# Activations in four parts by token number instead of two, in a float32 encoder kernel on one core

## What is computed

```python
for i in range(2):
    hn = _rms(h, norm_mix[i])
    h = h + (_even_mixer if i == 0 else _odd_mixer)(hn, ...)
    h = h + _conv_ffn(_rms(h, norm_ffn[i]), ...)
return h[:, N_META:]

def _conv_ffn(h, w_up, conv_w, conv_b, w_down):
    u = h @ w_up                      # 2048 -> 2 x 5632
    ...                               # a convolution over 3 neighbouring tokens
    g, val = jnp.split(acc, 2, axis=-1)
    return (jax.nn.silu(g) * val) @ w_down
```

## Time and profile before

| | us |
|---|---|
| time, median of 3 runs | 2368.8 (2368.6 to 2370.28) |
| the profiled execution's own time | 2367.88 |
| its span, first to last instruction | 2366.2 |
| TensorE busy / VectorE / ScalarE / GpSimd | 2335.8 / 1609.0 / 1185.0 / 51.8 |
| span up to the feed-forward part of layer 0 (first product of up00) | 476.4 |
| from there to layer 1 | 735.6 |
| mixer of layer 1 | 440.7 |
| feed-forward part of layer 1, with the output | 713.5 |

### The profile page before, as it was taken

How to read it: one execution, slowest core, us unless ns; L and a number is a source line. 1 busy time by engine, 2 the same in 40 slices (tenths; PEclk the granted TensorE clock), 3 DMA queues, 4 the chain that set the end, 5 groups by cost and what they waited for, 6 DMA issues and landing times.

```text
span 2366.2 us, 50508 instructions
## 1 busy us (share of the span) xinstructions
PE 2335.8 (99%) x19334; PEld 2278.9 (96%) x19334; DVE 1609.0 (68%) x2314; ACT 1185.0 (50%) x1592; POOL 51.8 (2%) x96
## 2 busy tenths in 40 slices
PE   8999999999999999999999999999999999999999
PEld 7999898999999999999999999999999999999998
DVE  5547786687755776577574667776877667766774
ACT  5345655554443544444459634455545445444543
POOL 0000011000000000000011000000000000000000
PEclk9999999999999999999999999999999999999999
DMA  6644465556566556655665544456566666566665
GB/s 194 189 143 130 134 160 139 181 166 206 182 195 190 184 178 197 195 186 184 192 187 159 159 119 121 139 177 198 179 193 197 213 190 197 183 215 189 199 202 163
DMA packets 431596, 420.25 MB, mean 178 GB/s; under 512 B 26130, under 2 KB 430396, under 8 KB 431452
## 3 DMA queue, kind: packets, MB, share of 16 engines
q1 hardware_dynamic: 417536, 415.29, 56.8%
q10 hardware_dynamic: 13932, 3.17, 1.2%
HBM read 416.31 MB, written 2.10 MB: 177 GB/s over the span
## 4 chain that ended last, share of the span: by engine, by line
PE 91%; DVE 4%; ACT 3%; issue 2%; ACTq 1%; DMA 0%; SPq 0%; DVEq 0%
PE ps L1533 28%; PE ps L1531 25%; PE ps L1532 25%; PE ps L1529 7%; PE ps L1768 1%; DVE w_lo L1023 1%; ACT w_hi L572 1%; PE ps L1762 1%; PE ps L1606 1%; PE ps L1608 1%; PE ps L1607 1%; ACTq L705 0%; PE ps L1566 0%; PE ps L1754 0%; ACT na_p L838 0%
## 5 line engine op out<-in xcount | busy, mean ns | idle before, releaser
L1531 PE MATMUL ps<-act_hi,w_hi 128*128 128x272 f32 (+1 forms) x4864 | 1367.3, 281 | 3.6 <-DVE w_lo L1023 3.6
L1532 PE MATMUL ps<-act_lo,w_hi 128*128 128x272 f32 (+1 forms) x4864 | 1350.9, 278 | 0.0
L1533 PE MATMUL ps<-act_hi,w_lo 128*128 128x272 f32 (+1 forms) x4864 | 1350.9, 278 | 0.0
L1023 DVE TENSOR_TENSOR w_lo<-raw,w_hi 128x1024 fp32r<-128x1024 f32 (+1 forms) x800 | 947.2, 1204 | 472.7 <-ACT w_hi L572 439.8
L572 ACT ACTIVATE w_hi<-raw 128x1024 fp32r<-128x1024 f32 (+1 forms) x796 | 814.4, 1035 | 680.5 <-PE ps L1533 641.4
L1531 PEld LDWEIGHTS ps<-act_hi,w_hi 128*128 128x128 f32 x4864 | 925.7, 190 | 7.3 <-DVE w_lo L1023 4.2
L1532 PEld LDWEIGHTS ps<-act_lo,w_hi 128*128 128x128 f32 x4864 | 925.7, 190 | 1.5
L1533 PEld LDWEIGHTS ps<-act_hi,w_lo 128*128 128x128 f32 x4864 | 925.3, 190 | 0.0
L1533 PE MATMUL ps<-g_both,w_lo 128*128 128x272 f32 (+1 forms) x1408 | 388.3, 276 | 0.0
L1533 PEld LDWEIGHTS ps<-g_both,w_lo 128*128 128x128 f32 x1408 | 268.2, 190 | 0.0
L1529 PE MATMUL ps<-g_both,w_hi 128*128 128x512 f32 x704 | 231.5, 383 | 0.0
(11 more groups left out here) (273 smaller groups left out, 1183.7 us busy)
## 6 DMA issues: line engine op xcount, KB each, us to landing
raw<-in_ffn_w_up SPq DMA_DIRECT2D x352, 512.0 KB, 4.6
raw<-in_ffn_w_down SPq DMA_DIRECT2D x128, 512.0 KB, 4.5
raw<-in_ab_w_in SPq DMA_DIRECT2D x96, 512.0 KB, 3.7
raw<-in_c_w_in SPq DMA_DIRECT2D x96, 512.0 KB, 3.8
raw<-in_ffn_w_down SPq DMA_DIRECT2D x64, 384.0 KB, 3.9
raw<-in_ab_w_out SPq DMA_DIRECT2D x32, 512.0 KB, 3.4
raw<-in_c_w_out SPq DMA_DIRECT2D x32, 512.0 KB, 4.4
tok<-in_x SPq DMA_DIRECT2D x8, 256.0 KB, 6.6
```

Of the source, the lines that this page charges most:

```text
L1023: V.tensor_tensor(w_lo[:, s % 4, 0:kc * 256], raw[:, s % 4, 0:kc * 256], w_hi[:, s % 4, 0:kc * 256].bitcast(F32), ALU.subtract).then_inc(S ...
L1531: mm(o, wh, moving(xh, kk), start=(c == 0 and k == 0), stop=False)
L1532: mm(o, wh, moving(xl, kk), start=False, stop=False)
L1533: ins = mm(o, wl, moving(xh, kk), start=False, stop=end)
```

## The change

The activations are stored in four parts, by token number modulo four. `parted` then reads its source at a step of four elements, each product reads the four parts in turn, and layer 1 leaves out 12 meta tokens in place of 14, since the first token kept must be a multiple of four: products of 258 columns become products of 260. The tiles keep their size, and no instruction is added or taken away.

```diff
-Q0 = META - 2
+Q0 = META - 4
-        act_hi = sb("act_hi", [P, KT, 2, T // 2], F32R)
-        act_lo = sb("act_lo", [P, KT, 2, T // 2], F32R)
+        act_hi = sb("act_hi", [P, KT, 4, T // 4], F32R)
+        act_lo = sb("act_lo", [P, KT, 4, T // 4], F32R)
-        g_both = sb("g_both", [P, MT, 2, 2, T // 2], F32R, at=zone)
+        g_both = sb("g_both", [P, MT, 2, 4, T // 4], F32R, at=zone)
@@ parted
-            return bass.AP(ap.tensor, ap.offset, dims + [[step, 2], [2 * step, n // 2]])
+            return bass.AP(ap.tensor, ap.offset, dims + [[step, 4], [4 * step, n // 4]])
@@ evac, the writers of g_hi and g_lo (high and low_gla of the mixer likewise, with Q0 // 4)
-                    high.append(chain.mark(V.tensor_copy(g_hi[:, bass.ds(i * 2 + m, 1), :, o0 // 2:], parted(gp[:, m:m + 1, o0:T]))))
+                    high.append(chain.mark(V.tensor_copy(g_hi[:, bass.ds(i * 2 + m, 1), :, o0 // 4:], parted(gp[:, m:m + 1, o0:T]))))
-                    ins = V.tensor_tensor(g_lo[:, k, :, o0 // 2:], parted(gp[:, m:m + 1, o0:T]),
-                                          g_hi[:, k, :, o0 // 2:].bitcast(F32), ALU.subtract)
+                    ins = V.tensor_tensor(g_lo[:, k, :, o0 // 4:], parted(gp[:, m:m + 1, o0:T]),
+                                          g_hi[:, k, :, o0 // 4:].bitcast(F32), ALU.subtract)
@@ moving, and the wide product
-                    return x_[:, kk, :, t0 // 2:].rearrange("p a b -> p b a")
+                    return x_[:, kk, :, t0 // 4:].rearrange("p a b -> p b a")
-                                mm(o2, wh, g_both[:, kk, :, :, t0 // 2:].rearrange("p c a b -> p c b a"), start=(c == 0 and k == 0), stop=False)
+                                mm(o2, wh, g_both[:, kk, :, :, t0 // 4:].rearrange("p c a b -> p c b a"), start=(c == 0 and k == 0), stop=False)
```

More of the change, by code:

```diff
@@ L976, in high @@
                 act.wait_ge(S("used"), 8 * (G["gl_out0"]["it0"] - 1) + 5 + k // 4)
-                A(act_hi[:, k, :, Q0 // 2:], parted(o_tile(k)[:, Q0:T]), ACT.Copy).then_inc(S("x_hi"), 1)
+                A(act_hi[:, k, :, Q0 // 4:], parted(o_tile(k)[:, Q0:T]), ACT.Copy).then_inc(S("x_hi"), 1)
             decay = decays()
@@ L1436, in low_gla @@
                 dve.wait_ge(S("x_hi"), 64 + k + 1)
-                V.tensor_tensor(act_lo[:, k, :, Q0 // 2:], parted(o_tile(k)[:, Q0:T]), act_hi[:, k, :, Q0 // 2:].bitcast(F32),
+                V.tensor_tensor(act_lo[:, k, :, Q0 // 4:], parted(o_tile(k)[:, Q0:T]), act_hi[:, k, :, Q0 // 4:].bitcast(F32),
                                 ALU.subtract).then_inc(S("act_ready"), 1)
```

## The result

The changed kernel takes 2888.6 us (median of 4 runs, 2887.1 to 2889.7), the kernel before 2368.7 in the same measurement: a ratio of 1.219, with a 95% interval from 1.217 to 1.221. It is slower, as forecast, but by 520 us and not by 31. The span is 2885.4 us. One of the six executions of the kernel with 266 columns, further down, took 3322 us at a mean granted clock of 0.69 and is left out of its comparison.

A forecast was written before the change was run, and what follows sets the result against it. The prediction took TensorE, 99% busy at its peak rate with VectorE close behind, as the bound. VectorE 24, columns 5.1, four parts 0 and other writers 2 made 31 us on 2367.9: 2399.5 us forecast, +1.3%, range 2370 to 2422.

The forecast's parts named there:

- Two columns more: Layer 1's 6,144 products go from 258 to 260 columns: 270 cycles with 10 over, +5.1 us.
- Four parts in turn: TensorE's 10,560 products of 272 columns read four parts at one column a cycle, as two parts: no cost, 0 us.
- the prediction's own last sentence: Wrong in size if the price is at an end, wrong in kind if TensorE's distance between products moves.
- theory L: From the experiments, not the prediction: four places crossing 16-byte lines within the same four columns make four parts dear.
- VectorE at 16 bytes: Four VectorE instructions before the split for step 3 grow about 0.25 us each; beyond the slack this adds 24 us.
- the split for step 3: VectorE's split of a tile after the long evac; TensorE needs it 0.61 us later in layer 0, where added time lands.
- the other writers: `norm_low`, the start reading from PSUM and ScalarE's reads: 2 us, between 0 and 6.
- Rival 1: VectorE reads one stepped source at full rate, so only the columns remain: 2374 us, or 2364 with 266 cycles; chance 0.12.
- Rival 2: Faster: four places shrink the gap between TensorE's products, all cycles over gone gives 2348 us; chance 0.06.
- Rival 3: A fixed 4 cycles in each TensorE product for opening four places; chance 0.06.
- the upper end of the columns: In the 260-column products, four parts starting on their last element of four: 6 + 8 over, 274 cycles, +15.4 us.
- Rival 4: TensorE pays the bystander's price at each column, 0.46 ns, some 4420 us; chance 0.04.

The follow-up runs named there:

- the kernel with 266 columns: The kernel before with 6 meta tokens left out in place of 14, still two parts: 2379.0 us, ratio 1.0045.
- the two small kernels: Separate kernels of nothing but 192 products of each reading pattern, the first also with copies and subtractions; 272 columns: two parts 278 cycles, four parts 348.
- with cheap writers: The changed kernel, four parts, but writers read their sources at 8 bytes in place of 16: 2889.6 us, ratio 1.2195.
- the small kernel: The first products-alone kernel, with copies and subtractions of 272 elements at several steps on VectorE and ScalarE: subtraction 442 ns dense, 632 with one source at 16 bytes.
- the second small kernel: Products alone again, each reading pattern on its own source line, with more distances, column counts and plain float32: 272 columns in two parts 278 cycles.
- the kernel with the slow writers: Two parts with 12 meta tokens left out, but writers read their sources at 16 bytes as in the change: 2391.1 us, ratio 1.0094.
- the kernel with cheap writers: The kernel before with 12 meta tokens left out in place of 14, two parts, writers at 8 bytes: 2369.8 us, ratio 1.0003.

## Why the prediction was wrong

**Two columns more.** "Take 10 over again" was a misreading. The 10 cycles are no surcharge on 258 columns; 268 is a floor under products in succession that each bring their own weights, here from 192 to 262 columns in two parts, whatever element they start at. Beyond it each column costs its cycle (262 columns 268, 266 columns 272, 268 columns 274, 272 columns 278), with 6 over. In two parts the term was +5.1 us and is 0. That the loading of the weights sets the floor is the author's guess and is not shown: no run keeps the weights in place. One sign of the floor stood in the trace of the kernel before, in the down products of layer 1, where products of 512 and 256 columns take turns:

```profile
2084.76 0.27 PE L1533 MATMUL ps<-g_both,w_lo 128*128 128x256 f32 x1
2084.87 0.38 PE L1529 MATMUL ps<-g_both,w_hi 128*128 128x512 f32 x1
2085.08 0.27 PE L1533 MATMUL ps<-g_both,w_lo 128*128 128x256 f32 x1
```

From the start of a product of 256 columns to the next start it is 109.2 ns on average, 262 cycles: below the floor, and the same 6 over as for 272 columns. Behind a long product the floor doesn't bind, so it isn't a cost of 258 columns as such.

**Four parts in turn.** This step failed: "For the 10,560 products I take no cost". The argument was that two parts already change place at each column at one column a cycle, so four would too. The runs show that it doesn't carry from two to four: 278 cycles become 348, both in the kernel and alone. The term was 0 for these 10,560 and measured 308 us; the 6,144 add 178 us and the wide ones, which "cost nothing by the same reasoning", 58. That is 544 us of product distance, 520 in the time. By the prediction's own last sentence this is wrong in kind and not only in size, since TensorE's distance between products moved. Under this step the choice between bounds was wrong as well. The row of a product that pays per column was at hand and was set aside because its places lie at another distance and its type is plain float32. Both reasons were true, and neither says that the nearer row is the safe one: two places and four are different questions. The text said that TensorE "is at its peak rate here". The runs bear that out as far as they go, for no order in the two small kernels took less than 0.417 ns for a column. But the right use of it was the opposite: an engine that is 99% busy with 278 cycles for 272 columns has no cover for any price per column, so a doubt there weighs 7 us for each cycle, many times a doubt about VectorE.

That the reading of four parts is the cause is shown: with cheap writers the time stays at 2889.6 us, two parts with 260 columns stay at 2369.8, and the products alone have the same 348 and 337 cycles. What makes four parts dear is shown only this far: with parts an even number of words apart they cost about a cycle for each four columns; an odd number apart and in the order of storage, 15 to 26 cycles a product; and in the kernel one word of padding gives 379 us back. A change of place at each column isn't dear as such: two parts change it each time and are the fastest of all kinds, 278 cycles against 303 for the dense run, which never does. Nor does the line of 16 bytes that theory L assumes show in the runs: the cheap distances, 276 to 340 bytes with 293 to 304 cycles, tell odd words from even ones and no more. Open are the mechanism inside, why the order 0, 2, 1, 3 undoes the padding, why 340 bytes cost 304, why six and eight parts cost more at any distance, and why plain float32 gains nothing from the padding.

**VectorE at 16 bytes.** That a source at a step of 16 bytes slows VectorE (a copy from 298 to 405 ns, a subtraction from 438 to 668) and that this reaches TensorE through the split for step 3 (6 waits, 7.9 us, where there were 3 with 3.6) is confirmed by itself: +21.3 us against a term of 24 + 2. That the sum agrees is luck: two errors cancel. The price was "0.93 ns an element" for each of the four instructions, 1.02 us an evac, and is 0.10 us for a copy and 0.19 to 0.23 for a subtraction, 0.63 an evac, so that the loops give 8 to 10 us in place of 21 (5.5 + 3.5 + 11.9). And the other writers, with 2 us, were sized too low: the waits around the first evacs and, in layer 0, the granted clock of 0.50 from 512.1 to 515.5 us, behind the longest of them, make some 7 us in place of these 2 and the 1.95 for the evacs themselves. That "an instruction can go no faster than its slowest stream" was the author's reason for this price, and no run shows it as a rule. What is shown is the subtraction of the small kernel: 442 ns dense, 632 with one source at 16 bytes, 641 with the output alone, 636 with both sources, 642 with all three. One stream, two or three cost 190 to 200 ns there, where 254 was taken from line 1375, which is another operation on another shape. For an element that is 0.70 ns in the subtraction and 0.36 in the copy (97 / 272), in place of 0.93. In the changed kernel the whole VectorE term is hidden, since the distance of 0.61 us grew to 2.13, and nothing of it is in the 520. The two more columns may be: once four parts are read, columns cost again (328 cycles for 256, 336 for 260 and 348 for 272 in the small kernel). An estimate from these is 2.5 to 4 cycles for two columns, 6 to 10 us on 6,144 products; four parts with 258 columns were not run. A slip that changes nothing: at half the price for VectorE the prediction's terms add up to 4 us and not to 5.

**The rivals.** Rival 1 falls, one stepped source pays (399 against 302 ns a copy). Rival 2 falls, the gap didn't shrink (145.0 ns a product in place of 115.8). Rival 3, a fixed 4 cycles in each product for opening four places, is wrong in kind: the price over two parts grows with the columns, from 0 at 200 columns, where the floor hides it, to 40 at 240 and 70 at 272. No run shows its 4 cycles either, which it took from where the 258 columns start, nor the 8 of the upper end of the columns: two parts of 256 to 262 columns take 268 cycles from each of seven starts. Rival 4 had the right engine, the right unit (per column) and four times too high a price; it had a chance of 0.04. Its hinge ("it would hang on the distance of the parts, which goes from 544 to 272 bytes") is half right: the distance counts, but four parts 544 bytes apart cost 349 cycles as well.

No version here beats the kernel before. Two parts have no surcharge in columns that could be taken back: 272 columns stand at 278 cycles, and 258 on the floor of 268.

## What to carry to other kernels

A rate measured with two interleaved places says nothing of four (278 against 348 cycles here); before the order of storage under a saturated TensorE is changed, time a couple of hundred products of the new reading alone and compare start-to-start distances, since durations overlap and hide it (313 ns long, 145.5 apart). If parts have to be read in turn, use two; if it must be four in float32r, pad each by one word and read them in the order of storage (2510 against 2889 us here). And when a short operation seems to pay a larger surcharge than a long one, suspect a floor: then a little more work in it is free (258, 260 and 262 columns all start 111.7 ns apart here).

## What the runs showed of the hardware

- Two interleaved parts feed TensorE better than a dense run: 278 against 303 cycles for 272 float32r columns, 2369 against 2523 us in the kernel. For plain float32 it is the other way, 692 against 550.
- With 192 to 262 columns in two parts, 128 to 240 dense or 192 to 200 in four parts, float32r products in succession with their own weights take 268 cycles each, 111.7 ns, so the reading costs nothing there; behind a product of 512 columns one of 256 takes 262.
- On VectorE a step of 8 bytes is free (302 and 442 ns, as dense), 12 bytes cost 39 ns in a copy of 272 elements, 16 bytes 97, and 32 bytes hardly more, 102. ScalarE pays earlier: 15 ns at 8 bytes, 131 at 12, 252 at 16.
- The clock: in the second small kernel, the products of 16 to 128 columns in two parts ran at a mean granted clock of 0.52, with TensorE busy throughout by the records; those of 64 and 128 columns start 213 ns apart. They are left out of the cycles above. The window (columns as above):

```profile
536.00:650.00 114.00, 114.00 (x559) 114.00 (x557) 0.00 (x0) 0.00 (x0) 0.00 (x0) 0.52 0.00 1
```

- After the stall of 2.55 us at 508.5 us in the kernel with the slow writers the granted clock stood at 0.50 from 512.1 to 515.5 us (products of 272 columns 227 ns apart in place of 115.8); the stall thus cost TensorE more than its own length. After the stall of 2.48 us at 1695.0 in the same kernel, and after the one of 1.2 us in the kernel with cheap writers, the products went on 112 and 116 ns apart at a granted clock of 1.00.
